# Chunked RWKV-7 recurrence: the 64x64 triangular inverse folded into 32x32 diagonal blocks

## What is computed

```python
def step(S, inp):
    r_t, w_t, k_t, v_t, a_t, b_t = inp
    sa = jnp.einsum('bhij,bhj->bhi', S, a_t)
    S = S * w_t[:, :, None, :] + sa[..., None] * b_t[:, :, None, :] + v_t[..., None] * k_t[:, :, None, :]
    y = jnp.einsum('bhij,bhj->bhi', S, r_t)
    return S, y
```

## Time and profile before

| | us |
|---|---|
| median of 3 runs | 1764.15 (1762.57 to 1768.33) |
| profiled execution, its own time | 1763.99 |
| its span, first to last instruction | 1762.2 |
| TensorE busy | 1649.7 (94%) |
| VectorE busy | 1295.3 (74%) |
| ScalarE busy | 1000.0 (57%) |
| recurrence, `first` of chunk 0 to `y` of chunk 4 | 135.4 (508.4 to 643.8) |
| mean granted TensorE clock | 0.955 |

### The profile page before, as it was taken

How to read it: one execution, slowest core, us unless ns; L and a number is a source line. 1 busy time by engine, 2 the same in 40 slices (tenths; PEclk the granted TensorE clock), 3 DMA queues, 4 the chain that set the end, 5 groups by cost and what they waited for, 6 DMA issues and landing times.

```text
span 1762.2 us, 29867 instructions
## 1 busy us (share of the span) xinstructions
PE 1649.7 (94%) x12114; PEld 1297.7 (74%) x12114; DVE 1295.3 (74%) x1256; ACT 1000.0 (57%) x1027; POOL 72.8 (4%) x111
## 2 busy tenths in 40 slices
PE   7778999989999996799999999999999999999995
PEld 6557999967889974777777777777777777777774
DVE  3655554465755425579899899898998998998984
ACT  3544443334802212367777777777777777777773
POOL 3000000000035300000000000000000000000000
PEclk9869999989989986899999999999999999999997
DMA  9412544621400001249999999999999999999980
GB/s 262 169 49 102 183 168 167 226 101 51 166 26 4 4 3 48 103 150 374 368 358 371 372 354 372 369 358 370 359 369 372 357 369 370 359 371 366 361 330 26
DMA packets 60292, 425.42 MB, mean 241 GB/s; under 512 B 6887, under 2 KB 8023, under 8 KB 9224
## 3 DMA queue, kind: packets, MB, share of 16 engines
q1 hardware_dynamic: 58152, 416.52, 62.6%
q0 software_dynamic: 2016, 7.13, 1.6%
HBM read 422.28 MB, written 1.12 MB: 240 GB/s over the span
## 4 chain that ended last, share of the span: by engine, by line
PE 71%; DVE 3%; ACT 2%; issue 1%; ACTq 0%; POOL 0%; DVEq 0%
PE PS L512 53%; PE PS L798 6%; PE PS L513 5%; PE PS L1012 1%; PE PS L814 1%; DVE arena L1364 1%; PE PS L968 1%; PE PS L823 1%; PE PS L552 1%; PE PS L998 0%; PE PS L999 0%; PE PS L558 0%; PE PS L936 0%; PE PS L776 0%; ACT h L1084 0%
## 5 line engine op out<-in xcount | busy, mean ns | idle before, releaser
L1364 DVE TENSOR_TENSOR w_lo<-ring,w_hi 128x2048 fp32r<-128x2048 f32 x395 | 903.3, 2288 | 208.9 <-ACT w_hi L1293 88.5
L1293 ACT ACTIVATE w_hi<-ring 128x2048 fp32r<-128x2048 f32 x336 | 644.7, 1919 | 264.3 <-PE PS L512 241.7
L512 PE MATMUL PS<-w_hi,x_hi 128*96 128x512 f32 x896 | 353.9, 395 | 0.7 <-ACT x_hi L1285 0.7
L512 PE MATMUL PS<-w_hi,x_lo 128*96 128x512 f32 x896 | 352.5, 393 | 0.0
L512 PE MATMUL PS<-w_lo,x_hi 128*96 128x512 f32 x896 | 243.0, 392 | 0.0
L1073 ACT ACTIVATE w_hi<-ring 128x2048 fp32r<-128x2048 f32 x59 | 112.9, 1914 | 168.2 <-issue 89.3
L512 PEld LDWEIGHTS PS<-w_lo,x_hi 128*96 128x96 f32 x896 | 144.6, 161 | 62.1
L512 PEld LDWEIGHTS PS<-w_hi,x_lo 128*96 128x96 f32 x896 | 144.8, 162 | 58.2
L512 PEld LDWEIGHTS PS<-w_hi,x_hi 128*96 128x96 f32 x896 | 144.6, 161 | 58.1 <-ACT x_hi L1285 1.0
L512 PE MATMUL PS<-w_hi,hid_hi 128*96 128x512 f32 x448 | 176.7, 394 | 0.0
L512 PE MATMUL PS<-w_hi,hid_lo 128*96 128x512 f32 x448 | 176.0, 393 | 0.0
(11 more groups left out here) (258 smaller groups left out, 2035.8 us busy)
## 6 DMA issues: line engine op xcount, KB each, us to landing
ring<-in_slabs SPq DMA_DIRECT2D x395, 1024.0 KB, 4.9
arena<-in_lora POOLq DMA_DIRECT2D x1, 1152.0 KB, 5.4
h<-in_h SPq DMA_DIRECT2D x1, 1088.0 KB, 6.6
arena<-bias_lines POOLq DMA_DIRECT2D x1, 1056.0 KB, 19.9
arena<-bias_lines POOLq DMA_DIRECT2D x1, 1040.0 KB, 24.6
arena<-in_lora POOLq DMA_DIRECT2D x1, 1024.0 KB, 12.0
out<-h SPq DMA_DIRECT2D x1, 1024.0 KB, 4.7
arena<-in_lora POOLq DMA_DIRECT2D x1, 512.0 KB, 6.5
```

Source lines behind the costliest of these rows:

```text
L512: return pe.matmul(out, x, w, start=start, stop=stop) if tokens_stay else \
L1293: act.activation(w_hi[:, n % 2, :], ring[:, n % SLOTS, :], ACT.Copy).then_inc(hi_set, 1)
L1364: tt = lambda o, a, b, op=ALU.mult: dve.tensor_tensor(out=o, in0=a, in1=b, op=op)
```

## The change

- The matrix is held folded: only the two diagonal 32x32 blocks of L, T and T transposed are kept (`lf`, `tf`, `ttf`, row r in partition r, column modulo 32). The levels 2, 4, 8 and 16 work on these blocks alone.
- New `per_block` (L790 to L803 of the changed kernel) issues, for each pair m, head p and block j, a matmul with 32 rows and 32 columns of the array: four tiles on the diagonal of the array instead of two. A half has 16 matmuls instead of 8.
- Level 32 joins the two blocks only: `u` from the off-diagonal block of L, then one product for the upper right block of T transposed (`xt`), and a copy of the lower block with an identity. ScalarE moves the result (`tr`), VectorE the first block (`tl`).
- L is made twice, as blocks of L and of L transposed (64 instead of 16 matmuls in a chunk of 64 tokens). ScalarE copies them (`lf`) and the values (`vnat`); VectorE's `vnat` copy and GpSimd's `ttm0`, `ttm` are gone. The elementwise steps of a level are half as wide.
- The last chunk of 16 tokens has one block, so its levels keep their number of matmuls; its L is made twice too.

```diff
-ON_SCALAR = ("um", "bk", "xm", "sam", "y")
-ON_GPSIMD = ("otm", "ttm0", "ttm")
+ON_SCALAR = ("lf", "vnat", "um", "tr", "bk", "xm", "sam", "y")
+ON_GPSIMD = ("otf",)
...
+            def per_block(g, b, lhsT, rhs, n, blocks, col=0, swap=False):
+
+                for m in range(4 * g, 4 * g + 4):
+                    at = col + FOLD * (m - 4 * g)
+                    for p in range(2):
+                        for j in blocks:
+                            o = 64 * p + FOLD * (1 - j if swap else j)
+                            mm = pe.matmul(PS[o:o + n, b + g, at:at + n], lhsT(m, p, j), rhs(m, p, j),
+                                           start=True, stop=True)
+                return mm
...
                     for g in range(2):
                         dv(g, "b_ra", c)
                         transposed(g, 0, 256, V, n)
-                        per_head(g, 0, n, n, (A, B))
+                        per_block(g, 0, A_blocks, B_blocks, nf, blocks)
+                        per_block(g, 0, B_blocks, A_blocks, nf, blocks, col=128).then_inc(c_pe, 1)
...
-                        per_head(g, 0, n, n, (by_token(otm[levels % 2], c, n), by_token(tm[q], c, n)))
+                        if LEVELS[i] < FOLD:
+                            dv(g, "otf", c, i)
+                            per_block(g, 0, block_of(otf[i], nf), t_, nf, blocks).then_inc(c_pe, 1)
+                        else:
+                            across = lambda m, p, j: ltm[q][64 * p:64 * p + FOLD, m, FOLD:2 * FOLD]
+                            per_block(g, 0, across, t_, nf, (0,), swap=True).then_inc(c_pe, 1)
                     for g in range(2):
-                        if i == 0:
-                            dv(g, "ttm", c)
                         dv(g, "um", c, i)
+                        if LEVELS[i] == FOLD:
+                            eye_ = lambda m, p, j: masks[64 * p + FOLD:64 * p + 64, MASKS.index("eye64"), FOLD:2 * FOLD]
+                            per_block(g, 2, um_, tt_, nf, (1,), swap=True)
+                            per_block(g, 2, eye_, tt_, nf, (1,)).then_inc(c_pe, 1)
+                            continue
                         if i < last:
-                            per_head(g, 2, n, n, (ttc, by_token(um, c, n)))
-                        per_head(g, 2, n, n, (by_token(um, c, n), ttc), col=256)
-                    levels = levels + 1
+                            per_block(g, 2, tt_, um_, nf, blocks).then_inc(c_pe, 1)
+                        per_block(g, 2, um_, tt_, nf, blocks, col=128).then_inc(c_pe, 1)
```

More of the change, by code:

```diff
@@ L91, in recurrence_order @@
         parts["first", c] = (halves(["b_ra", "k_ra", "l_v"] + more, c),
[L92 to L96, removed]
+                             halves(["b_ra", "k_ra", "lf", "vnat"] + more + ["t0", "t1"], c))
+        for i, b in enumerate(levels_of(c)):
+            if b == FOLD:
+                parts["level", c, i] = halves(["u"], c, i) + halves(["xt"], c, i), halves(["um", "tl", "tr"], c, i)
+            else:
+                both = ("tu", "tut") if i < len(levels_of(c)) - 1 else ("tut",)
+                parts["level", c, i] = (halves(["u"], c, i) + [(x, c, i, g) for g in range(2) for x in both],
+                                        halves(["otf", "um", "t+"], c, i))
         parts["x", c] = halves(["x"], c), halves(["xm"], c)
@@ L154 @@
 EARLY = 2
-MASKS = ["low2", "low2T", "upper_eq", "upper"] + [f"off{b}" for b in LEVELS] + ["eye64"]
+MASKS = ["low2", "upper_eq", "upper", "off2", "off8", "eye32", "first", "eye64"]
 def build(nc, A, OUT):
@@ L464, in _ @@
             order, PT, DV, AV, PV = recurrence_order()
-            levels_done = []
             for part, c, *level in order:
[L467 to L473, removed]
+                n = min(FOLD, tokens_of(c))
+                if part == "level" and LEVELS[level[0]] < FOLD:
+                    i = level[0]
+                    off = folded(("off2", "off8")[i // 2], n)[:, i % 2:i % 2 + 1, :].broadcast_to([P, KC // 2, n])
                     for g in range(2):
                         at = (slice(None), slice(4 * g, 4 * g + 4), slice(0, n))
[L476 to L491, removed]
+                        pool.wait_ge(c_act, AV["lf", c, 0, g])
+                        pool.tensor_tensor(out=otf[i][at], in0=lf[:, 1][at], in1=off, op=ALU.mult).then_inc(c_pool, 1)
                 elif part == "x" and c == 0:
@@ L1241, in _ @@
                 name = {"x": "x", "sa": "sa", "y": "y", "level": "u", "first": "bk"}.get(part)
+                nf = min(FOLD, n)
+                if part == "first":
+                    for g in range(2):
+                        act.wait_ge(c_pe, PT["l_v", c, 0, g])
+                        act.activation(lf[:, :, 4 * g:4 * g + 4, 0:nf],
+                                       PS[:, g, 0:256].rearrange("p (k m t) -> p k m t", k=2, m=4)[:, :, :, 0:nf],
+                                       ACT.Copy).then_inc(c_act, 1)
+                    for g in range(2):
+                        act.activation(vnat[q][:, 4 * g:4 * g + 4, :],
+                                       PS[:, g, 256:512].rearrange("p (m t) -> p m t", m=4), ACT.Copy).then_inc(c_act, 1)
+                    kept = kept + 4
                 if at is None or part == "first" and c == N_CH - 1:
@@ L1252, in _ @@
                     elif part == "level":
-                        out, rows = um[:, heads, 0:n], rows[:, :, 0:n]
+                        out = um[:, heads, 0:nf]
+                        rows = PS[:, g, 0:128].rearrange("p (m t) -> p m t", m=4)[:, :, 0:nf]
                     elif part == "y":
@@ L1259, in _ @@
                     kept = kept + 1
+                if part == "level" and LEVELS[i] == FOLD:
+                    for g in range(2):
+                        act.wait_ge(c_pe, PT["xt", c, i, g])
+                        act.activation(ttm[q][:, 4 * g:4 * g + 4, FOLD:2 * FOLD],
+                                       PS[:, 2 + g, 0:128].rearrange("p (m t) -> p m t", m=4), ACT.Copy).then_inc(c_act, 1)
+                    kept = kept + 2
             assert kept == len(AV)
@@ L1648, in _ @@
                                     masks[:, at:at + 2, 0:n].unsqueeze(2).broadcast_to(wide)))
-                    both("l_v", tm[q], 0, mask("low2", n))
-                    both(None, tm[q], tm[q], mask("eye64", n), ALU.add)
+                    nf = min(FOLD, n)
+                    for name, x, op in (("low2", lf, ALU.mult), ("eye32", t_both, ALU.add)):
+                        for g in range(2):
+                            dve.wait_ge(c_act, AV["lf", c, 0, g])
+                            begin()
+                            t = (slice(None), slice(None), slice(4 * g, 4 * g + 4), slice(0, nf))
+                            step(tt(t_both[t], x[t], folded(name, nf).unsqueeze(2).broadcast_to([P, 2, KC // 2, nf]), op))
+                elif part == "level" and LEVELS[i] == FOLD:
                     for g in range(2):
                         begin()
-                        step(dve.tensor_copy(vnat[q][:, 4 * g:4 * g + 4, :],
-                                             PS[:, g, 256:512].rearrange("p (m t) -> p m t", m=4)))
+                        step(dve.tensor_scalar(ttm[q][:, 4 * g:4 * g + 4, 0:FOLD], ttf[:, 4 * g:4 * g + 4, :],
+                                               masks[:, MASKS.index("first"), 0:1], None, ALU.mult))
                 elif part == "level":
+                    nf = min(FOLD, n)
                     kinds = slice(0, 2) if i < len(levels_of(c)) - 1 else slice(1, 2)
```

52 lines of the change are left out of this document (34 added, 18 removed).

## The result

| | before | after |
|---|---|---|
| median us | 1763.86 (4 runs, 1762.57 to 1768.33) | 1816.57 (4 runs, 1813.7 to 1818.88) |
| ratio | | 1.0296 (1.0277 to 1.0315) |
| recurrence, us | 135.4 | 188.0 |
| mean granted TensorE clock | 0.955 | 0.929 |

A forecast was written before the change was run, and what follows sets the result against it. TensorE's queue was taken to bound the recurrence, each block of 256 instructions costing a 3.8 us fetch. Blocks +53 us and low clock +14 us made +67 us on 1763.99 us: 1831 us, range 1795 to 1868 us.

The forecast's parts named there:

- both terms of the sum: Recurrence: +53 us for instruction blocks and +14 us for the lower TensorE clock, together +67 us.
- The bound: Recurrence: TensorE's queue bounds the stage, so the change costs a price per TensorE record.
- Number of blocks: Recurrence: 1040 more matmuls, 4160 instructions, take 31.1 blocks of 256 instructions to 47.4.
- The timing of a fetch: TensorE's instruction queue: a fetch begins 1.1 us after a block is begun, and the engine goes on 2.6 us later.
- Blocks term: Recurrence: 47.4 blocks at 3.8 us, 180 us, plus 8 us for slow blocks, against 135.4 us: +53 us.
- the 8 us added for slow blocks: Blocks slower than a fetch: 6 us for `with_r_kk` in four chunks, some 2 us for chunk 4's last products.
- Those last products: End of chunk 4: 96 records in 4.81 us, slower than a fetch by themselves, adding some 2 us.
- What folding gains, 2 us a period: L and levels, if fetched in time: 992 small records, 12.8 us, in place of 512 records, 14.9 us.
- Clock term: 64- and 128-column records: low clock costs 11.5 us a period, 46 us for four; low 30% of the time, +14 us.
- Rival 1: TensorE's queue: the fetch is no limit, small records take 12.4 to 16.2 ns; 1753 us, faster; chance 0.08.
- Rival 2: TensorE's array: four tiles do not run beside each other, small records take 29 ns, blocks in time; 1818 us; chance 0.07.
- Rival 3: Recurrence: starved blocks and shorter chains cancel, so the change does little; needs 2.9 us a block; chance 0.03.

The follow-up runs named there:

- e7: Changed kernel with each small matmul of levels 2 to 16 streaming its 32 columns four times over, same instructions and results: 1806.99 us, ratio 1.0261.
- e1: Kernel before with an extra 16-column matmul, stationary 64 rows and 16 wide, ahead of each 64x64 one of the levels: 1956.54 us, ratio 1.1081.
- e2: Changed kernel with only the first 32x32 block of each pair in L and levels 2 to 16, 896 matmuls fewer: 1761.15 us, ratio 0.9991.
- e1b: Kernel before with an extra 16-column matmul, stationary 64 wide like its neighbours, ahead of each 64x64 one of the levels: 1808.41 us, ratio 1.0266.
- e6: Changed kernel with one 128x128 block-diagonal matmul for the four 32x32 blocks in the levels of the 64-token chunks: 1886.05 us, ratio 1.0696.

## Why the prediction was right, and where its terms were off

1831 us were forecast and 1816.57 measured, in the range and on the forecast side, with the cause that was named. Of the +67 us 53 came: both terms of the sum were too large.

- **The bound.** TensorE's queue, and a price per record, not VectorE's or ScalarE's chain: held. `t+` takes 421 ns as read from the earlier trace rows, and its waits lie inside the blocks.
- **Number of blocks.** 4160 instructions more, 47.4 blocks forecast, 47.3 counted, 48 packets. The timing of a fetch, 1.1 and 2.6 us, held as well (1.0 to 1.4 and 2.4 to 2.9 us in chunk 0).
- **Blocks term, +53 us.** The pace of 3.8 us itself was good as a mean: five starved blocks of chunk 0 lie 18.89 / 5 = 3.78 us apart, and the stage has 188.0 / 47.3 = 3.97 us a block in the changed kernel and 3.81 with the clock full up to chunk 4 (e7). As a floor, "3.7 us at least", it was too high: 3.38 us in chunk 0, 3.58 over three blocks of e7. With e7's clock the stage is 180 us, and +45 is the term's right size. What failed is the 8 us added for slow blocks. A block with the 64 records of `with_r_kk` and 64 small ones takes 3.5 + 0.9 = 4.4 us by itself, 0.6 more than 3.8 and not 1.5; this is argued from rows, not tried.
- **Those last products.** The 50 ns a record of the earlier trace rows were taken as the price of that work. Of these 96 records 64 alternate, in groups of four, between stationaries of 64 and of 16 rows, and half of the stretch ran at the low clock. e1 shows that a change of width costs time; that a change of height does was not tried alone.
- **What folding gains, 2 us a period.** It did not come. A period of the kernel before has 240 matmuls in L and the levels (16, four times 48, and 32), 480 records and not the 512 of the prediction, 14.0 us. The 992 small ones take 14.1 to 15.1 ns in bursts and not 12.4, 14.0 to 15.0 us. At the array the change gains nothing.
- **Clock term, +14 us.** The clock did fall, for longer than the 30% assumed (about 98 of 188 us, 52%), and cost less, an estimated 3 to 10 us. What failed is the price at the low level: 11.5 us a period had every block of 64-column records take its full 7.5 us. These records do run at half pace then (64 in 3.61 us, against 1.87 in the earlier trace rows), but the fetch goes on meanwhile, and behind such a stretch the chain runs on without a gap for 7 to 8 us (from 587.05 to 594.64, from 630.38 to 638.30). `with_r_kk`, charged with 3.4 us more a period, took 3.71 to 4.46 us in place of 3.50. Where TensorE starves, the clock is mostly hidden; where it does not, as in e1, it costs in full.
- **Rival 1** (fetch no limit, 1753 us) fell: a gap at each of the six block boundaries from 519 to 538 us and 31 gaps for 47 blocks in all, and fewer instructions take the loss away (e2). Half of its reasoning was right, for in bursts the small records do take 14 to 15 ns (96 in 1.35 us, and 128 in 1.93 us at the low clock). The Trainium skill ("Runtime: NRT & Kernel Launch", "Instruction fetch mechanics") calls the crossing of a block mostly hidden; this trace disagrees, with 1.4 to 2.1 us at each in chunk 0.
- **Rival 2** (tiles not side by side, 1818 us) has nearly the measured time and is wrong: e7's 0.22 ns a column, and the bursts. The time alone could not have told it from the forecast.
- **Rival 3** (little change) needed 2.9 us a block. No stage had less than 3.81 in the mean.

So the change halved each product's time at the array and doubled their number, which comes to nothing there, and the supply of instructions made it 53 us slower. The kernel before sits where three paces meet, all of 27 to 30 ns a record: 64 columns streamed, 64-wide float32 weights loaded (argued by elimination), 256 instructions fetched. No variant here that does the whole work beats it. What stays open: whether the fetch can be asked for earlier, and an inverse with fewer products in all, which would serve all three; neither was tried.

## What to carry to other kernels

Count TensorE's instructions in the stage, divide by 256 and multiply by 3.8 to 4.0 us (here); when the engine's own time comes below that, shorter or narrower matmuls gain nothing and more of them cost 30 ns a record. Compare the number of matmuls with the time of each before packing into smaller tiles: here one doubled as the other halved. Keep neighbouring matmuls in one tile size, and look at the weight load of a float32 stationary before widening it.

## What the runs showed of the hardware that was not expected

- A change of tile size between neighbouring matmuls costs at least 85 ns at full clock (0.41 against 0.24 us for eight records, two changes), if the narrower weights load no slower.
- A record with a 64-wide float32 stationary, two tiles side by side, took 29 ns even with 16 columns (e1b); a 32-wide one took 18.8 ns in two tiles (e2) and 14 to 15 in four, and one 128 wide 128 ns at the full clock and 207 at the low one (e6).
- TensorE starved by its instruction queue at the low clock for half of a stage lost only an estimated 3 to 10 us of 188 by that clock.
- With four tiles of 32x32, four times the columns were 6 to 10 us faster than the columns needed, and the clock was full then until chunk 4.
